# Pairs of heads in a two-block kernel: state steps 1 to 6 in place of 0 to 7, and VectorE's mean and variance of the last pair behind the level's subtractions

## The chip, the cores and the metric

The kernel runs on one core of one Trainium2 chip. The metric is the device time of one execution in microseconds (us); the median of three runs is given. TensorE is PE in the profile (PEld is its weight loads), VectorE is DVE, ScalarE is ACT, GpSimd is POOL, SyncE is SP.

## What is computed

`x` (1, 256, 2048) goes through two layers of a first block (gated linear attention, gated delta rule, differential attention) and then through a second block. The second block mixes its tokens by three parts side by side, and the first of them, 16 heads of 64 channels, is what the change touches. It scans the context (256 tokens) and then the sequence (256 tokens), forwards and backwards, all in float32:

```
def step(s, inp):
    r_t, w_t, k_t, v_t, kk_t, a_t = inp
    sa = jnp.einsum('bhij,bhj->bhi', s, -kk_t)
    s = (s * w_t[:, :, None, :] + sa[..., None] * (kk_t * a_t)[:, :, None, :]
         + v_t[..., None] * k_t[:, :, None, :])
    return s, jnp.einsum('bhij,bhj->bhi', s, r_t)
...
y = yf + yb
mu = jnp.mean(y, axis=-1, keepdims=True)
var = jnp.mean(jnp.square(y - mu), axis=-1, keepdims=True)
y = ((y - mu) * lax.rsqrt(var + GN_EPS) * ln_w + ln_b)
y = y + jnp.sum(r * (kf + kb) * r_k, axis=-1, keepdims=True) * v
return y * (jax.nn.sigmoid(gd) @ g_up), (sf, sb)
```

The context's scan starts from a state of zeros; the sequence's scan starts from the context's last state. Only the sequence's `y` is used. An output projection, a gated feed-forward part and a last norm follow.

## The kernel before

The second block's heads are worked off two at a time: `NP2 = 8` turns `j`, one for each pair, in five hand-written programs (`pairs_pe`, `pairs_act`, `pairs_dve` and parts of the POOL and SP programs) that run side by side and meet in semaphores. Every engine runs its own program in the written order, so an instruction that waits holds all that is written behind it on its engine. `d` is the direction (0 forwards, 1 backwards).

The 512 tokens of a pair are eight cells of 64, cells 0 to 3 of the context and 4 to 7 of the sequence, in the order of the direction. One turn does, in this order:

- **levels 1 to 5**: the inverse of each cell's triangular matrix, by doubling. For each level PE multiplies masks by the inverse so far (line 1843, "the first products"), ACT copies the result, PE multiplies again (lines 1856 and 1858, "the second products"), and DVE subtracts the result from the inverse and its transpose (lines 2517 and 2518, for each of the two directions: four subtractions a level). POOL makes the masks of levels 2 to 5 (line 1472).
- **the last pair's end**: `y` of pair `j - 1` is finished between the levels of turn `j`. PE's `head_means` (lines 1866 to 1869) stands behind level 1 and `head_vars` (line 1874) behind level 2. On DVE `centred` (it subtracts the mean; lines 2523 and 2525, the first shown as L2436) stands ahead of level 1's subtractions, `variances` (line 2530) ahead of level 2's, and `normed` (lines 2535 to 2541) ahead of level 3's. On ACT `squares` (line 2150) stands behind the copies of level 1 and `head_roots` (line 2154) behind those of level 2. POOL loads the pair's gate weights (line 1463) when `normed` is done, and makes the masks of levels 4 and 5 behind that.
- **`solved` and `steps`**: for each cell the matrix `step` and the addend `Z` of the state's recurrence.
- **the states**: a chain over cells. `GS[m + 1] = decay[m] * (step[m] x GS[m]) + Z[m]`. PE's `state(j, m)` is four products (two halves for each direction, line 1939), DVE's `state(j, m)` two small instructions (line 2564, shown as L2436 with 128x64). There are eight such steps, m = 0 to 7; `GS[0]` is set to zero by a memset on DVE (line 2556).
- **the next pair's streams**: DVE makes the backward inputs of pair `j + 1` in six parts (`stream(j + 1, 1, part)`), one behind each of the state's steps 0 to 5; the last part is line 2487. PE turns these inputs by `by_token(j + 1, r)` (lines 1788 and 1789): r = 0 and 1 stand behind steps 1 and 3, r = 2 behind the last step, r = 3 behind `outputs`. r = 2 needs the part of line 2487.
- **`outputs`**: PE multiplies `GS[4]` to `GS[7]` by the queries (line 1949), DVE gathers `y` (lines 2572 and 2574).

The last turn (j = 7) has no next pair. It has instead four large DVE sums over the mixed rows (`mix_sums`, lines 2332 to 2337) behind level 3's subtractions.

Of the kernel before, what the change touches and what calls it, by code (L numbers as in the profile page):

```python
# [1254 lines left out]
def second_block(nc, ctx, A, B, out):  # L1255
# [489 lines left out]
    def pairs_pe(pe):  # L1745
# [189 lines left out]
        def state(j, m):  # L1935
            for d in range(2):
                need("p_state", j, count(m + 1, d))
                for hs in halves:
                    mm = pe.matmul(PS[hs, d, cell(m)], step[d][hs, m, :], GS[d][hs, m, :], start=True, stop=True)
                done(mm, "p_gs")  # L1940

        def outputs(j):
            need("p_ypre", j, 1)
            for d in range(2):
                need("p_state", j, count(9, d))
# [15 lines left out]
        for j in range(NP2):  # L1961
# [461 lines left out]
    def pairs_dve(v, mix_sums):  # L2423
# [452 lines left out]
```

How the kernel before makes its waits and increments, by code:

```python
    def need(self, sig, k):  # L193
        self.eng.wait_ge(sig.sem, k + sig.start if self.turn is None else sig.at(self.turn, k))
# [6 lines left out]
    def settle(self):  # L201
        self.eng.wait_ge(self.last.sem, self.last.start + self.mark)
# [92 lines left out]
    def sp_program(sp):  # L296
        for n in range(NMOD1):
            if n >= RING:
                sp.wait_ge(vec_done.sem, n - RING + 1)
            sp.dma_start(ring[:, n % RING].rearrange("p k n -> p (k n)"), A["w_start"][n]).then_inc(opened[n % RING].sem, 16)
            if n % 2 == 0:
                i = n // 2
                if i > 1:
                    sp.wait_ge(S("aside_used").sem, i - 1)
                load[i % 2].inc(sp.dma_start(aside(i).rearrange("p c t n -> p (c t n)"), A["w_aside"][i]), 16)
        for l in range(NL):
            for t in range(0 if l else NSIDE, TILES1):
                if l or t > NSIDE + 1:
                    sp.wait_ge(tiles_done.sem, tiles_done.at(l, t - 1))
                else:
                    sp.wait_ge(vec_done.sem, (16, 14)[t % 2])
                load[t % 2].inc(sp.dma_start(ring[:, t % 2].rearrange("p k n -> p (k n)"), A["w_first"][l][t]), 16)
# [2 lines left out]
    def pool_program(pool):  # L315
# [8 lines left out]
        for l in range(NL):  # L324
            for i in range(VEC0[l], VEC0[l + 1]):
                pool.wait_ge(vec_done.sem, vec_done.start + (-1 if i < 2 else i - 2 if l == 0 else max(i - 1, VEC0[1])))
                half_loaded[half_place(i)].inc(pool.dma_start(half_slot(i), A["w_vec"][i]), 16)
```

## Time and profile before

| | us |
|---|---|
| median of 3 runs | 3397.76 (3395.79 to 3398.54) |
| the profiled execution, its own time | 3396.16 |
| its span in the trace | 3394.3 |
| the eight turns, in the trace | about 1855 to 2406, some 550 of the span |
| PE busy, share of the span | 92% |
| DVE busy | 47% |
| ACT busy | 16% |
| POOL busy | 33% |

The first block ends and the second block's input products run before the turns; its output projection and feed-forward part run behind them, with PE busy in nine tenths or more. In the turns PE is busy in seven to eight tenths, and they move next to nothing from memory. A turn takes some 70 us. Times of the trace are counted from the start of the span.

### The profile page before, as it was taken

How to read it: one execution, taken by the hardware profiler on the slowest of the kernel's cores; microseconds unless marked ns; L12 is line 12 of the kernel's file. 1: busy time of each engine (PE TensorE's matmuls, PEld its weight loads, DVE VectorE, ACT ScalarE, POOL GpSimd, SP SyncE). 2: the span in 40 equal slices, each digit the busy share in tenths (PEclk: the TensorE clock that was granted, in tenths of full speed). 3: DMA queues.
4: the chain of work that ended last, by engine and by line, in shares of the span. 5: the costliest groups of instructions: out<-in, count | busy, mean ns of one | idle time of the engine just before them, and what ended most of it. 6: DMA issues, size and time to landing. Idle time of an engine off the chain costs nothing.

```text
span 3394.3 us, 69586 instructions
## 1 busy us (share of the span) xinstructions
PE 3112.3 (92%) x32190; PEld 2794.7 (82%) x32190; DVE 1596.5 (47%) x2384; ACT 544.6 (16%) x1022; POOL 1109.8 (33%) x621
## 2 busy tenths in 40 slices
PE   5998999998999999999896888777999999999998
PEld 4877887877878888687895777666889999999998
DVE  4745275455437610587814666666334442113111
ACT  1012112021210111100003443343010000000001
POOL 1000000000000010243671211112447797778774
PEclk8998999998999999999997999999899999999999
DMA  7955387765335643477640000000445654444443
GB/s 281 405 224 198 120 316 286 306 246 205 107 145 216 231 177 139 172 274 288 250 150 11 10 7 7 7 7 6 162 149 224 227 221 170 161 167 162 162 166 109
DMA packets 56035, 583.10 MB, mean 172 GB/s; under 512 B 7314, under 2 KB 9680, under 8 KB 10816
## 3 DMA queue, kind: packets, MB, share of 16 engines
q1 hardware_dynamic: 37808, 465.06, 36.7%
q0 software_dynamic: 17936, 113.59, 8.8%
q8 instruction: 253, 4.15, 0.5%
q14 instruction: 38, 0.31, 0.0%
HBM read 576.52 MB, written 2.10 MB: 170 GB/s over the span
## 4 chain that ended last, share of the span: by engine, by line
PE 70%; DVE 13%; DMA 9%; issue 3%; ACT 3%; POOL 2%; SPq 0%; ACTq 0%; DVEq 0%; POOLq 0%
PE PS L1675 24%; PE PS L374 14%; PE PS L672 7%; PE PS L1628 5%; DMA ring<-in_w_vec_dram 5%; DMA ring<-in_w_second_dram 2%; DVE ring L2244 2%; PE PS L417 2%; PE PS L1843 1%; DMA ring<-in_w_start_dram 1%; PE PS L371 1%; PE PS L1856 1%; PE PS L1692 1%; PE PS L1611 1%; PE PS L1888 1%
## 5 line engine op out<-in xcount | busy, mean ns | idle before, releaser
L374 PE MATMUL PS<-H,ring 128*128 128x256 f32 x2944 | 669.4, 386 | 7.0 <-ACT H L702 7.0
L374 PEld LDWEIGHTS PS<-H,ring 128*128 128x128 f32 x2944 | 562.6, 193 | 95.0 <-issue 17.6
L1675 PE MATMUL PS<-H,ring 128*128 128x128 f32 x3424 | 404.5, 276 | 1.5 <-DMA ring<-in_w_second_dram 1.5
L1675 PEld LDWEIGHTS PS<-H,ring 128*128 128x128 f32 x3424 | 394.7, 193 | 2.4 <-DMA ring<-in_w_second_dram 1.9
L2351 DVE TENSOR_TENSOR W<-W,PS 128x256 f32<-128x256 f32 x58 | 24.4, 421 | 679.8 <-ACT W L2001 679.7
L327 POOL DMA_DIRECT2D ring<-in_w_vec_dram x75 | 39.7, 530 | 923.9 <-DVE ring L888 785.7
L1675 PE MATMUL PS<-H,W 128*128 128x128 f32 x2624 | 316.6, 276 | 8.4 <-POOL W L1504 7.2
L1675 PEld LDWEIGHTS PS<-H,W 128*128 128x128 f32 x2624 | 305.0, 193 | 9.7 <-POOL W L1504 8.0
L1499 POOL TENSOR_TENSOR W<-ring 128x1024 f32<-128x1024 f32 (+1 forms) x74 | 179.7, 2429 | 265.7 <-PE PS L1675 149.2
L672 PE MATMUL PS<-H,ring 128*128 128x256 f32 x1024 | 223.5, 379 | 2.9 <-DVE H L1174 2.9
L672 PEld LDWEIGHTS PS<-H,ring 128*128 128x128 f32 x1024 | 194.2, 190 | 29.9 <-issue 3.7
L1472 POOL TENSOR_TENSOR ring<-ring,W 128x512 f32<-128x512 f32 x64 | 84.9, 1342 | 367.1 <-PE PS L1843 366.7
L888 DVE SCALAR_TENSOR_TENSOR ring<-ring,H 128x2048 f32<-128x2048 f32 x75 | 171.1, 2287 | 29.3 <-DMA ring<-in_w_vec_dram 28.6
L1504 POOL TENSOR_TENSOR W<-ring,W 128x1024 f32<-128x1024 f32 (+1 forms) x74 | 182.4, 2465 | 5.8
L1502 POOL TENSOR_TENSOR W<-W,ring 128x1024 f32<-128x1024 f32 (+1 forms) x74 | 181.6, 2455 | 0.0
L1501 POOL TENSOR_TENSOR ring<-ring 128x1024 f32<-128x1024 f32 (+1 forms) x74 | 177.4, 2398 | 5.8
L1628 PE MATMUL PS<-H,ring 128*128 128x128 f32 (+1 forms) x992 | 142.5, 306 | 9.8 <-DMA ring<-in_w_second_dram 4.9
L1628 PEld LDWEIGHTS PS<-H,ring 128*128 128x128 f32 x992 | 134.4, 199 | 16.5 <-issue 5.7
L2244 DVE SCALAR_TENSOR_TENSOR ring<-ring,W 128x2048 f32<-128x2048 f32 x48 | 127.2, 2666 | 38.5 <-DMA ring<-in_w_vec_dram 38.0
L2001 ACT ACTIVATE W<-PS 128x128 f32<-128x128 f32 (+2 forms) x61 | 18.6, 307 | 786.1 <-PE PS L1675 777.3
L1675 PE MATMUL PS<-Pj,ring 128*128 128x128 f32 x1184 | 139.8, 275 | 3.3 <-DVE H L2337 3.3
L1675 PEld LDWEIGHTS PS<-Pj,ring 128*128 128x128 f32 x1184 | 135.9, 192 | 3.5 <-issue 3.5
(500 smaller groups left out, 4990.5 us busy)
## 6 DMA issues: line engine op xcount, KB each, us to landing
ring<-in_w_second_dram SPq DMA_DIRECT2D x97, 2048.0 KB, 8.1
ring<-in_w_first_dram SPq DMA_DIRECT2D x68, 2048.0 KB, 8.3
ring<-in_w_vec_dram POOLq DMA_DIRECT2D x75, 1024.0 KB, 7.8
ring<-in_w_vec_dram SPq DMA_DIRECT2D x48, 1024.0 KB, 5.1
ring<-in_w_start_dram SPq DMA_DIRECT2D x16, 2048.0 KB, 15.7
H<-in_w_vec_dram POOLq DMA_DIRECT2D x21, 1024.0 KB, 8.1
Pj<-in_w_aside_dram SPq DMA_DIRECT2D x8, 2048.0 KB, 11.2
ring<-in_w_second_dram SPq DMA_DIRECT2D x9, 1536.0 KB, 6.6
```

What stands on the lines that cost most here:

```text
L374: mm = pe.matmul(PS[:, t % 2, half * T:(half + 1) * T], ring[:, t % 2, k, half * P:(half + 1) * P], hT[:, k, :], start=(k == 0), stop=(k = ...
L417: mm = pe.matmul(PS[:, t, half * T:(half + 1) * T], left, right, start=(k == 0 and half == 0), stop=(k == KC - 1), skip_group_check=True)
L672: mm = pe.matmul(PS[:, 4 + 2 * (n % 2) + half, 0:T], ring[:, t % 2, k, half * P:(half + 1) * P], hT[:, k, :], start=(k == 0), stop=(k == K ...
L888: return v.scalar_tensor_tensor(out, a, s, b, op0, op1, **kw)
L1472: S("p_mask").inc(pool.tensor_tensor(mT[d], aT[d], Ci(f"c_join{lev}").unsqueeze(1).to_broadcast([P, 8, CH]), ALU.mult))
L1499: sums.inc(pool.tensor_tensor(s_[:, 0], quarter(q, 2, nk), quarter(q, 3, nk), ALU.add))
L1501: sums.inc(pool.tensor_tensor(quarter(q, 2, nk), quarter(q, 0, nk), quarter(q, 2, nk), ALU.subtract))
L1502: sums.inc(pool.tensor_tensor(s_[:, 1], s_[:, 0], quarter(q, 0, nk), ALU.subtract))
L1504: sums.inc(pool.tensor_tensor(s_[:, 2], quarter(q, 1, nk), s_[:, 1], ALU.subtract))
L1628: mm = pe.matmul(in_regions(n % 2, wide, r), w[:, k * P:(k + 1) * P], at(m, k), start=(k == 0 and r // per not in opened), stop=(k == 7), ...
L1675: mm = pe.matmul(regions(bank2, r), w[:, k * P:(k + 1) * P], m[:, k, :], start=(first and k == 0 and r // 4 not in opened), stop=(last and ...
L2244: v.scalar_tensor_tensor(w, w, 1.0, crow2[:, 0, :], ALU.mult, ALU.mult, accum_out=mod2[:, i - 64, 0:1]).then_inc(vec_done.sem, 1)
```

## The change

The state's steps 0 and 7 are left out. `GS[0]` is zero, so step 0 gives `GS[1] = Z[0]`: PE's step 1 reads `Z[0]` directly, and DVE's memset and its step 0 go. Step 7 gives `GS[8]`, which nothing reads. Six steps are left, m = 1 to 6; the six parts of the next pair's stream stand behind them one by one, `by_token` 0 and 1 behind the second and the fourth of them, and `by_token` 2 behind the last.

On DVE `centred` moves from ahead of level 1's subtractions to behind them, and `variances` from ahead of level 2's to behind them. PE's, ACT's and POOL's programs keep their order.

```diff
         def state(j, m):
             for d in range(2):
-                need("p_state", j, count(m + 1, d))
+                if m > 1:
+                    need("p_state", j, count(m - 1, d))
                 for hs in halves:
-                    mm = pe.matmul(PS[hs, d, cell(m)], step[d][hs, m, :], GS[d][hs, m, :], start=True, stop=True)
+                    mm = pe.matmul(PS[hs, d, cell(m)], step[d][hs, m, :], GS[d][hs, m, :] if m > 1 else Z[d][hs, 0, :], start=True, stop=True)
                 done(mm, "p_gs")
...
         def outputs(j):
             need("p_ypre", j, 1)
             for d in range(2):
-                need("p_state", j, count(9, d))
+                need("p_state", j, count(6, d))
...
             steps(j)
-            for m in range(8):
+            for m in range(1, 7):
                 state(j, m)
-                if after and m in (1, 3):
-                    by_token(j + 1, m // 2)
+                if after and m in (2, 4):
+                    by_token(j + 1, m // 2 - 1)
             if after:
                 by_token(j + 1, 2)
...
-            o.do(v.memset(GS[d][:, 0, :], 0.0), S("p_state"))
             need("p_reff", j, d + 1)
...
         def state(j, m):
             o = Order(v, own, j)
             for d in range(2):
-                need("p_gs", j, count(m + 1, d))
+                need("p_gs", j, count(m, d))
...
             starts(j)
+            level(j, 1)
             if before:
                 centred(j - 1)
-            level(j, 1)
+            level(j, 2)
             if before:
                 variances(j - 1)
-            level(j, 2)
...
-            for m in range(8):
+            for m in range(1, 7):
                 state(j, m)
-                if after and m < 6:
-                    stream(j + 1, 1, m)
+                if after:
+                    stream(j + 1, 1, m - 1)
```

The diff also changes the two counts of a turn that the semaphores of these steps reach. Lines behind 1937 are one higher in the changed kernel, up to the memset that is gone.

The order of VectorE from the end of level 1's starting values to level 2's subtractions, in a turn that has a pair before it. Before (`centred` is the pair of rows L2436 and L2525, `variances` L2530, the subtractions L2517 and L2518):

```order
L2504 TENSOR_TENSOR ring<-PS,W 128x512
L2436 SCALAR_TENSOR_TENSOR Pj<-PS,Pj 128x256
L2525 TENSOR_TENSOR Pj<-PS,Pj 128x256
L2517 TENSOR_TENSOR ring<-ring,PS 128x512
L2518 TENSOR_TENSOR ring<-ring,PS 128x512
L2517 TENSOR_TENSOR ring<-ring,PS 128x512
L2518 TENSOR_TENSOR ring<-ring,PS 128x512
L2530 TENSOR_SCALAR Pj<-PS 128x256
L2517 TENSOR_TENSOR ring<-ring,PS 128x512
L2518 TENSOR_TENSOR ring<-ring,PS 128x512
```

In the changed kernel (the same instructions, lines one higher):

```order
L2505 TENSOR_TENSOR ring<-PS,W 128x512
L2518 TENSOR_TENSOR ring<-ring,PS 128x512
L2519 TENSOR_TENSOR ring<-ring,PS 128x512
L2518 TENSOR_TENSOR ring<-ring,PS 128x512
L2519 TENSOR_TENSOR ring<-ring,PS 128x512
L2437 SCALAR_TENSOR_TENSOR Pj<-PS,Pj 128x256
L2526 TENSOR_TENSOR Pj<-PS,Pj 128x256
L2518 TENSOR_TENSOR ring<-ring,PS 128x512
L2519 TENSOR_TENSOR ring<-ring,PS 128x512
L2518 TENSOR_TENSOR ring<-ring,PS 128x512
L2519 TENSOR_TENSOR ring<-ring,PS 128x512
L2531 TENSOR_SCALAR Pj<-PS 128x256
```

`centred` and `variances` each moved behind four subtractions; nothing else on VectorE moved there.

VectorE at the end of the state's chain, in a turn with a next pair. Before (the 128x64 rows are the state's steps, L2480 to L2487 parts 3 to 5 of the next pair's stream, L2572 the start of `outputs`):

```order
L2480 TENSOR_TENSOR W<-W 128x512
L2436 SCALAR_TENSOR_TENSOR Pj<-PS,H,ring 128x64
L2436 SCALAR_TENSOR_TENSOR H<-PS,H,ring 128x64
L2482 TENSOR_TENSOR Pj<-W,Pj 128x256
L2483 COPY H<-W 128x8
L2436 SCALAR_TENSOR_TENSOR Pj<-PS,H,ring 128x64
L2436 SCALAR_TENSOR_TENSOR H<-PS,H,ring 128x64
L2487 TENSOR_TENSOR W<-W 128x512
L2436 SCALAR_TENSOR_TENSOR Pj<-PS,H,ring 128x64
L2436 SCALAR_TENSOR_TENSOR H<-PS,H,ring 128x64
L2436 SCALAR_TENSOR_TENSOR Pj<-PS,H,ring 128x64
L2436 SCALAR_TENSOR_TENSOR H<-PS,H,ring 128x64
```

In the changed kernel:

```order
L2481 TENSOR_TENSOR W<-W 128x512
L2437 SCALAR_TENSOR_TENSOR Pj<-PS,H,ring 128x64
L2437 SCALAR_TENSOR_TENSOR H<-PS,H,ring 128x64
L2483 TENSOR_TENSOR Pj<-W,Pj 128x256
L2484 COPY H<-W 128x8
L2437 SCALAR_TENSOR_TENSOR Pj<-PS,H,ring 128x64
L2437 SCALAR_TENSOR_TENSOR H<-PS,H,ring 128x64
L2488 TENSOR_TENSOR W<-W 128x512
L2572 COPY Pj<-PS 128x2x2x64
```

The four rows behind the stream's last part are gone: that part, and no longer a step of the state, is now the last thing ahead of `outputs`.

## Rows read from the trace of the kernel before

**Rows 1.** The page: the span.

```profile
span 3394.3 us, 69586 instructions
```

**Rows 2.** Three windows: length; busy PE, PEld, DVE, ACT, POOL; clock; DMA share; GB/s.

```profile
1925.00:1995.00 70.00, 56.24 (x1794) 48.79 (x1794) 46.67 (x96) 28.44 (x52) 12.43 (x11) 0.98 0.03 8
2135.00:2206.00 71.00, 58.84 (x1796) 51.47 (x1795) 46.63 (x96) 28.48 (x52) 12.55 (x11) 0.92 0.03 8
2346.00:2410.00 64.00, 46.91 (x1246) 40.34 (x1245) 37.15 (x72) 12.27 (x25) 9.85 (x7) 0.84 0.21 80
```

**Rows 3.** Waits in the turns: who waited, for whom, us in total, times, longest.

```profile
PE PS L1843 <- DVE ring L2517: 18.0, 15, 2.6
...
PE PS L1858 <- issue: 8.3, 9, 2.0
PE PS L1856 <- issue: 7.6, 8, 1.3
```

**Rows 4.** Timeline of PE, levels 1 to 3 of turn 3: start, us, instruction, wait before it.

```profile
2063.10 1.03 PE L1869 MATMUL PS<-Pj,W 128*128 128x256 f32 x4
2065.79 2.29 PE L1843 MATMUL PS<-ring 64*64 64x64 f32 x62 [1.66 <-DVE ring L2517]
...
2070.49 0.70 PE L1874 MATMUL PS<-Pj,con 128*128 128x256 f32 x2
2071.03 0.95 PE L1768 MATMUL PS<-con,W 128*128 128x2 f32 x8
2072.39 0.29 PE L1843 MATMUL PS<-ring 64*64 64x64 f32 x3 [0.42 <-DVE ring L2517]
```

**Rows 5.** Timeline of DVE in the same stretch.

```profile
2064.16 0.42 DVE L2436 SCALAR_TENSOR_TENSOR Pj<-PS,Pj 128x256 f32<-128x256 f32 x1 [4.91 <-PE PS L1869]
...
2071.23 0.42 DVE L2530 TENSOR_SCALAR Pj<-PS 128x256 f32<-128x256 f32 x1 [3.79 <-PE PS L1874]
...
2076.85 0.42 DVE L2541 TENSOR_TENSOR H<-Pj,PS 128x256 f32<-128x256 f32 x1
```

**Rows 6.** Timeline of ACT in that stretch, and of POOL.

```profile
2064.62 0.42 ACT L2097 ACTIVATE Pj<-Pj 128x256 f32<-128x256 f32 x1 [6.41 <-DVE Pj L2436]
2066.98 0.60 ACT L2097 ACTIVATE ring<-PS 128x512 f32<-128x512 f32 x1 [1.94 <-PE PS L1843]
...
2071.68 0.42 ACT L2097 ACTIVATE Pj<-Pj 128x256 f32<-128x256 f32 x1 [1.61 <-DVE Pj L2530]
2073.58 0.60 ACT L2097 ACTIVATE ring<-PS 128x512 f32<-128x512 f32 x1 [1.48 <-PE PS L1843]
```

```profile
2077.57 0.75 POOL L1463 DMA_DIRECT2D W<-in_g_up_dram  x1 [8.04 <-DVE H L2541]
2078.34 2.50 POOL L1472 TENSOR_TENSOR ring<-ring,W 128x512 f32<-128x512 f32 x2
```

**Rows 7.** Timelines of DVE and PE, end of the state's chain in turn 3.

```profile
2111.15 0.68 DVE L2487 TENSOR_TENSOR W<-W 128x512 f32<-128x512 f32 x1
...
2112.67 0.27 DVE L2436 SCALAR_TENSOR_TENSOR H<-PS,H,ring 128x64 f32<-128x64 f32 x1
```

```profile
2112.09 0.33 PE L1939 MATMUL PS<-Pj,ring 64*64 64x64 f32 x4 [0.46 <-DVE Pj L2436]
...
2112.54 0.33 PE L1788 MATMUL PS<-con,W 128*128 128x128 f32 x1
```

**Rows 8.** Timeline of PE in the last turn: waits of levels 3 and 4, end of the chain.

```profile
2355.95 2.29 PE L1843 MATMUL PS<-ring 64*64 64x64 f32 x62 [1.20 <-DVE ring L2517]
...
2363.16 2.31 PE L1843 MATMUL PS<-ring 64*64 64x64 f32 x62 [2.26 <-POOL ring L1472]
...
2391.72 0.33 PE L1939 MATMUL PS<-Pj,ring 64*64 64x64 f32 x4 [0.20 <-DVE Pj L2436]
...
2392.44 0.33 PE L1939 MATMUL PS<-Pj,ring 64*64 64x64 f32 x4 [0.19 <-DVE Pj L2436]
...
2394.98 1.12 PE L1949 MATMUL PS<-Pj 64*64 64x64 f32 x16 [0.27 <-DVE Pj L2436]
```

More of the change, by code:

```diff
@@ new lines @@
+PER_TURN = {'load0': 304, 'load1': 304, 'load2': 0, 'tiles_done': 38, 'evac0': 19, 'evac1': 19, 'pair_end': 1, 'vec_done': 48, 'half0_loaded': 304, 'half1_loaded': 296, 'half2_loaded': 168, 'open0_loaded': 0, 'open1_loaded': 0, 'open2_loaded': 0, 'in_loaded': 16, 'aside_used': 0, 'dl_out': 1, 'p_y': 2, 'y_scaled': 2, 'out_stored': 64, 'y_scaled_act': 2, 'const_loaded': 16, 'c_loaded': 16, 'pos_loaded': 16, 'small_loaded': 320, 'heads_loaded': 64, 'wsm_loaded': 32, 'wlr_loaded': 16, 'narrow': 1, 'crow_loaded': 0, 'mix_ready': 4, 'ctx_loaded': 16, 'rows_zero': 1, 'vec_loaded': 352, 'c2_loaded': 16, 'at_rec': 2, 'ff_sum': 372, 'h_scaled': 16, 'h_scaled_2': 32, 'mix_rest': 4, 'cells_loaded': 16, 'pair_loaded': 32, 'gla_z': 1, 'p_z': 2, 'dl_P0': 6, 'p_P': 10, 'gla_ln': 1, 'p_mask': 8, 'gate_loaded': 16, 'at_root': 2, 'ff_t': 2, 'c3_loaded': 16, 'x_T': 8, 'x_copied_dve': 4, 'x_copied_act': 4, 'vcol_T': 0, 'x_sq': 8, 'x_ssq': 1, 'h_ready': 16, 'lam_prod': 1, 'lam_sum': 1, 'nar_copied': 1, 'nar_T': 1, 'gla_kt': 1, 'gla_ktT': 1, 'gla_scores': 1, 'dl_glog': 1, 'dl_gcum': 1, 'gla_ktok': 1, 'gla_ds': 1, 'gla_att': 1, 'gla_state': 1, 'gla_out': 1, 'dl_ug': 1, 'dl_rows': 1, 'dl_sq': 4, 'gla_norm_in': 1, 'dl_ssq': 1, 'dl_rec': 1, 'dl_brow': 2, 'dl_nb': 1, 'dl_kb': 1, 'dl_kk': 1, 'dl_vs': 2, 'dl_vT': 1, 'dl_aT': 1, 'dl_vtok': 1, 'dl_A': 1, 'dl_kT': 1, 'dl_af': 2, 'dl_x0': 1, 'dl_mT0': 5, 'dl_mT1': 5, 'dl_P1': 6, 'dl_Pc0': 6, 'dl_Y0': 6, 'dl_Pc1': 6, 'dl_Y1': 6, 'dl_inv': 12, 'dl_v0': 1, 'dl_v0c': 1, 'dl_s1': 1, 'dl_s1c': 1, 'dl_ks': 1, 'dl_r1': 1, 'dl_v1': 1, 'dl_v1c': 1, 'o_sq': 2, 'o_ssq': 2, 'o_rec': 2, 'o_nb': 2, 'at_sq': 2, 'at_ssq': 2, 'o_normed': 1, 'at_nb': 2, 'at_normed': 2, 'at_rope': 1, 'at_scores': 8, 'at_max': 8, 'at_a': 4, 'at_aT': 4, 'at_aTc': 4, 'at_out': 4, 'sq_2': 24, 'ctx_T': 8, 'ctx_copied': 8, 'vec_T': 1, 'csq_2': 1, 'ssq_2': 4, 'h_ready_2': 32, 'in_t': 2, 'mod_done': 1, 'ft_1': 1, 'at_ms': 2, 'ft_copied': 2, 'ft_2': 1, 'lora_act': 2, 'p_ksq': 1, 'p_kssq': 1, 'dl_ms': 1, 'p_kms': 1, 'dl_dec': 1, 'p_sig': 4, 'gla_zb': 1, 'p_kbig': 1, 'p_kbc': 1, 'p_streams': 2, 'p_tokT': 4, 'p_tokc': 4, 'p_AX': 2, 'p_BR': 2, 'p_mT': 2, 'p_xt': 1, 'p_BRr': 2, 'p_Pc': 10, 'p_x0': 2, 'p_Y': 10, 'at_exp': 16, 'p_xm': 8, 'p_sub': 10, 'p_bv': 2, 'p_bvc': 4, 'p_u': 2, 'p_uc': 4, 'p_g': 2, 'p_rhs': 2, 'p_kk': 1, 'p_reff': 2, 'p_Zread': 2, 'p_rt': 2, 'p_ypre': 1, 'p_step': 2, 'p_gs': 12, 'p_state': 12, 'p_yread': 2, 'p_ysum': 1, 'p_mean': 1, 'dl_outc': 1, 'p_ysq': 1, 'p_var': 1, 'p_bg_read': 1, 'down_t': 3, 'y_ready': 8, 'y_T': 8, 'down_read': 8, 'out_turned': 8, 'act_start': 25, 'c_done': 1, 'ang_red': 2, 'rope_abs': 2, 'act_step': 29, 'x_ms': 1, 'x_root': 1, 'lam_exp': 1, 'gb_copied': 1, 'dl_z': 1, 'dl_ebeta': 1, 'dl_ln': 1, 'gla_cum': 1, 'gla_blast': 1, 'gla_exps': 8, 'dl_gcr': 2, 'dl_eg': 2, 'dl_diff': 1, 'dl_root': 1, 'o_ms': 2, 'o_root': 2, 'c_next': 0, 'c_last': 1, 'ms_2': 4, 'root_2': 4, 'c_scaled': 1, 'ff_first': 77, 'in_conv': 11, 'mix_ft': 1, 'p_act': 14, 'p_kroot': 1, 'p_krec': 1, 'p_tm': 2, 'p_cs': 2, 'p_exp': 2, 'p_yc': 1, 'p_vms': 1, 'p_vroot': 1, 'x_new': 16, 'c_again': 1, 'ff_prod': 22, 'ff_silu': 21, 'rs_ready': 1, 'dve_start': 393, 'dve_step': 200, 'vec_copied': 4, 'p_dve': 28, 'p_ak': 2, 'p_kd': 2, 'p_bonus': 2}
```

1 line of the change is left out of this document (removed).

## The prediction

> **What bounds the kernel now.** I read the page first: the span is 3394.3 us, and the execution's own time 3396.16 lies 1.9 above it [rows 1]. The median of the runs shown, 3397.76, lies 1.6 above the profiled execution. Then the windows of single turns: PE is busy for 56.24 of 70 us, DVE for 46.67, ACT for 28.44, and memory moves 8 GB/s [rows 2]. So no engine is full in the turns; they are a chain that passes from engine to engine, and what counts is which wait ends last at each place. The list of waits names the one that the change touches most: PE's first products of a level wait 18.0 us for DVE's subtractions [rows 3]. The timelines then say what DVE was doing while PE waited.
>
> **Part 1, `centred` behind level 1's subtractions.** In turn 3 PE ends `head_means` at 2063.10 + 1.03 = 2064.13 and then stands for 1.66 us until DVE has subtracted [rows 4]. DVE had nothing to do for 4.91 us before `centred`, since `centred` waits for `head_means` and the subtractions are queued behind it [rows 5]; their own input, level 1's second products, stands ahead of `head_means` on PE. With the subtractions first they run inside those 4.91 us (four, of which `centred`'s end at 2065.04 and PE's start at 2065.79 bound the first at 0.75), and PE goes from `head_means` straight into level 2: 1.66 us gone. Who waits for the moved `centred`? It starts when `head_means` ends, as now. ACT's `squares` runs at 2064.62 + 0.42 = 2065.04 and the first copy of level 2, queued behind it, is wanted when PE's first half of level 2 is done. That copy now starts at 2066.98 [rows 6], so with PE 1.66 earlier at 2065.32: 0.28 us of room. Cost nothing, and at most some tenths if that room is used up.
>
> **Part 2, `variances` behind level 2's subtractions.** DVE waits 3.79 us for `head_vars` with level 2's subtractions behind it [rows 5], and PE, done with `head_vars` and the next pair's key sums at 2071.98, waits 0.42 us for the first of them [rows 4]. That goes. What is late next: `variances` follows the subtractions; the second products of level 2 end near `head_vars`' start, 2070.49 - 1.66 = 2068.83, two subtractions follow to about 2070.1, then `variances` to 2070.5, and ACT's root to 2071.0. That root stands ahead of ACT's copies of level 3, whose first is now at 2073.58 [rows 6] and would be wanted at 2073.58 - 2.08 = 2071.50: 0.5 us of room. DVE's `normed` follows the root; from the root's end 2071.68 + 0.42 = 2072.10 to the end of `normed`, 2077.27, there are 5.2 us today, of which DVE spends the first 1.9 on level 2's subtractions, which will lie ahead of it. It would end at 2071.0 + 3.3 = 2074.3, 2.9 us earlier than now. POOL's gate load and first mask of level 4 hang on it: 2077.57 to 2078.34 + 1.25 = 2079.6 today [rows 6], about 2076.7 then, against level 4's start that only moves by 2.08. So POOL's cover grows.
>
> **Sum of parts 1 and 2.** The 15 waits of 18.0 us are seven of 1.66, six of 0.42 (turns 1 to 6), 1.20 in the last turn at level 3, and one of about 2.6 at level 5 of the last turn behind `mix_sums`, which stays. Removed: 7 x 1.66 + 6 x 0.42 + 1.20 = 15.3 us. In the last turn level 4 waits 2.26 us for POOL's mask [rows 8]; the mask hangs on `normed`, which moves by the same 2.9 us as PE, so the gain is kept, and `mix_sums` starts as much earlier.
>
> **Part 3, six state steps.** In a turn with a next pair the last step's DVE instruction ends at 2112.67 + 0.27 = 2112.94, two steps of about 0.85 us behind the stream's last part [rows 7]. One would think that 1.7 us go. But the six stream parts still stand one behind each of six steps, so the last part still ends where it ends now, at 2111.15 + 0.68 = 2111.83, and PE's `by_token` 2, written ahead of `outputs`, needs it. Today `by_token` 2 starts at 2112.54 [rows 7]; it will start at about 2111.89 (DVE's end plus the 0.06 us by which PE follows DVE in these steps). Gain 0.65 us in each of seven turns, 4.5 us. The rest of the removed steps was, and will be, beside the stream. The last turn has no stream: its steps follow each other at 0.72 us, one at 2391.72, the sixth at 2392.44, and from there to `outputs` at 2394.98 are 2.54 us for three steps' DVE part and two steps' PE part [rows 8]. Two steps of 0.72 are 1.44; the remaining 1.1 can't all be the last DVE instruction, whose start is about 0.8 behind its PE part, so these steps ran slower than 0.72 each. Gain between 1.4 and 1.8 us, I take 1.6. Sum 6.1 us.
>
> **Part 4, small ones.** The two memsets per turn stand in DVE's queue ahead of a wait, and DVE starts the next instruction 0.03 us behind each; 0.2 us over the kernel, between 0 and 0.9. PE's eight fewer products per turn (each stands as two matmuls and two weight loads in the trace) lie in stretches where PE waits for DVE: nothing. Reading `Z` in place of `GS` adds no wait, since PE's last wait before the chain is for DVE's instruction that stands behind it.
>
> **What eats into the sum.** PE also stands for "issue", with no releaser: 8.3 us in 9 places on line 1858 and 7.6 in 8 on line 1856 [rows 3], the second products, where its instructions are shortest. Where a stop fell inside a wait that goes now, it shows. I take 1 us, between 0 and one such stop (0.9 us) per turn, 7 us. [...]
>
> **The sum.** 15.3 + 6.1 + 0.2 - 1 = 20.6 us. Against the profiled execution 3396.16 - 20.6 = 3375.6; against the median 3397.76 - 20.6 = 3377.2. I predict 3377 us, 0.6% less.
>
> **Rivals.**
> (a) The waits come back as stops. One more stop of 0.9 us per turn, or POOL's masks holding level 4: if the root on ACT came so late that `normed` did not move, level 4's mask would end at 2079.6 as now, where PE would want it at 2077.9, and most of the 2.08 us of a turn were lost. For it: only 0.28 and 0.5 us of room on ACT. Against it: `normed` is worked out 2.9 us earlier. Time 3384 to 3390.
> [...]
> [...]
> (d) It does not do what it says: `head_means`, and not DVE, is what level 2 waits for. Then part 1 gives nothing: 3377 + 11.6 = 3389. But PE's row says DVE for all 1.66 us.
>
> **How the numbers follow.** Forecast, 3372 to 3382: 0.66. (a) and (d), 3382 to 3391: 0.17. (b), under 3372: 0.10. Within 0.2% of before (6.8 us, about what a measurement of this kernel can tell from no change), from (a) with (c) partly: 0.04. (c): 0.03. Faster by over 0.2% is then 0.93, same 0.04, slower 0.03. The range takes (b)'s time and half of (a): 3369 to 3387.
>
> **What would show it.** In the changed kernel PE's wait ahead of level 2's first products is gone behind `head_means` (under 0.2 us), and that of level 3 too; `by_token` 2 starts right behind the end of the stream's last part; ACT's `squares` and root stand before the copies without PE waiting for them; the last turn has `outputs` about 1 us behind its sixth step. A turn is 67.3 us long where its clock is 0.98. The prediction is wrong if "issue" on lines 1856 and 1858 grows by more than 5 us, if PE waits for ACT at levels 2 or 3, or if the turns' mean clock changes by more than 0.02.

## The result: 36.9 us less, where 20.6 were forecast

The changed kernel takes 3361.3 us (median of 4 runs, 3359.2 to 3364.0), the kernel before in the same comparison 3398.2 us: a ratio of 0.9892, 95% interval 0.9875 to 0.9909. The direction was forecast, the size was not: 3377 was said, and 3361.3 lies below the range of 3369 to 3387. The spans of the two profiled executions differ by the same 36.9 us, 3394.3 [rows 1] and, on the page of the changed kernel:

```profile
span 3357.4 us, 69274 instructions
```

Nearly the whole difference, 35.0 us, arises in the turns. From the first product of `scores` of the first pair to the first product behind the turns the kernel before takes 562.3 us and the changed kernel 527.3. What lies ahead of them is the same work in both and is 3.1 us shorter in this pair of profiles (1842.8 and 1839.7 us); what lies behind is 989.2 us in the one and 990.4 in the other. The windows of that stage (columns as in [rows 2]), the kernel before first, then the changed kernel:

```profile
1842.80:2405.10 562.30, 449.92 (x14297) 393.93 (x14296) 366.96 (x745) 213.24 (x391) 98.74 (x84) 0.95 0.04 12
```

```profile
1839.70:2367.00 527.30, 438.65 (x14169) 386.58 (x14168) 361.99 (x698) 213.85 (x391) 98.34 (x84) 0.95 0.04 13
```

In this pair of profiles the granted clock is 0.95 in both, 57 us at the lower of its two levels before and 53 after; more runs show a larger difference (see "The clock" below). The two levels are 1.00 and 0.50: the granted clock is 1.00 over 2346 to 2356 us of the kernel before and 0.50 over 2394 to 2398. Line 1869's four matmuls take 1.03 us at the upper level [rows 4] and 1.91 us at the lower (at 2400.26). PE is busy for 11.3 us less although only 128 small matmuls (of 14,297) are gone, and it stands still for 23.7 us less.

The list of PE's waits in the turns of the changed kernel, to be held against [rows 3] (who waited, for whom, us in total, times, longest):

```profile
PE PS L1856 <- DVE ring L2437: 19.1, 8, 2.4
PE PS L1788 <- DVE W L2488: 8.3, 7, 1.2
...
PE PS L1843 <- POOL ring L1472: 5.2, 7, 3.0
...
PE PS L1843 <- DVE ring L2518: 3.1, 1, 3.1
...
PE PS L1856 <- issue: 2.8, 5, 1.4
```

The wait of the first products for DVE has one case left, the one of level 5 in the last turn behind `mix_sums` (2.6 us before, 3.1 now); 14 of 15 are gone. "Issue" on line 1856 fell from 7.6 to 2.8 us, and line 1858 is not in the list of the changed kernel at all (8.3 us before). These are the stops that the prediction expected to grow. On some other lines "issue" did grow: from 2.6 to 4.5 us on line 1829 and from 1.3 to 3.9 on line 1908. The wait for POOL's masks grew too; before, its row was:

```profile
PE PS L1843 <- POOL ring L1472: 3.0, 3, 2.3
```

Turn 3 of the changed kernel on PE, levels 1 to 4, against [rows 4]:

```profile
2050.71 1.03 PE L1869 MATMUL PS<-Pj,W 128*128 128x256 f32 x4
2051.67 2.08 PE L1843 MATMUL PS<-ring 64*64 64x64 f32 x63
...
2055.96 0.70 PE L1874 MATMUL PS<-Pj,con 128*128 128x256 f32 x2
2056.50 0.95 PE L1768 MATMUL PS<-con,W 128*128 128x2 f32 x8
2057.38 2.08 PE L1843 MATMUL PS<-ring 64*64 64x64 f32 x63
...
2063.85 1.15 PE L1843 MATMUL PS<-ring 64*64 64x64 f32 x32 [0.35 <-POOL ring L1472]
```

Level 2's first products follow `head_means` with no wait, level 3's follow the key sums with none. Two things beside that were not in the forecast. The group of first products, 62 matmuls in 2.29 us before, is 63 in 2.08 us now. And level 4 waits 0.35 us for POOL.

DVE in that stretch, against [rows 5]:

```profile
2049.84 0.69 DVE L2518 TENSOR_TENSOR ring<-ring,PS 128x512 f32<-128x512 f32 x1 [0.42 <-PE PS L1858]
2050.44 0.68 DVE L2519 TENSOR_TENSOR ring<-ring,PS 128x512 f32<-128x512 f32 x1
2051.78 0.42 DVE L2437 SCALAR_TENSOR_TENSOR Pj<-PS,Pj 128x256 f32<-128x256 f32 x1 [0.66 <-PE PS L1869]
```

The four subtractions now lie in what was idle time, and `centred` still starts as `head_means` ends. At the chain's end (against [rows 7]), DVE and then PE:

```profile
2095.68 0.68 DVE L2488 TENSOR_TENSOR W<-W 128x512 f32<-128x512 f32 x1
```

```profile
2096.42 0.33 PE L1788 MATMUL PS<-con,W 128*128 128x128 f32 x1 [1.19 <-DVE W L2488]
```

`by_token` 2 starts 0.06 us behind the end of the stream's last part, as worked out. In the last turn (against [rows 8]) the sixth step and `outputs` are 0.81 us apart:

```profile
2356.29 0.33 PE L1940 MATMUL PS<-Pj,ring 64*64 64x64 f32 x4 [0.19 <-DVE Pj L2437]
...
2357.10 1.12 PE L1950 MATMUL PS<-Pj 64*64 64x64 f32 x16 [0.28 <-DVE Pj L2437]
```

So every wait that should go went, and 14 to 16 us more went than was forecast. The experiments look for those.

### The profile page after: what moved, and what is told of

Read it like the earlier page. It is cut to its first block, busy times and chain, and to the rows that moved or that the text cites. A ratio compares the mean times of both kernels' runs of the same rounds, so it can differ in the third digit from the quotient of the medians.

```text
span 3357.4 us, 69274 instructions
## 1 busy us (share of the span) xinstructions
PE 3095.8 (92%) x32062; PEld 2782.9 (83%) x32062; DVE 1601.0 (48%) x2336; ACT 545.2 (16%) x1022; POOL 1106.2 (33%) x621
## 3 DMA queue, kind: packets, MB, share of 16 engines
q1 hardware_dynamic: 37808, 465.06, 36.9%
## 4 chain that ended last, share of the span: by engine, by line
PE 69%; DVE 14%; DMA 9%; ACT 3%; issue 3%; POOL 2%; SPq 0%; ACTq 0%; DVEq 0%; POOLq 0%
PE PS L1675 24%; PE PS L374 14%; PE PS L672 7%; DMA ring<-in_w_vec_dram 5%; PE PS L1628 5%; PE PS L417 2%; DMA ring<-in_w_second_dram 2%; DVE ring L2245 2%; PE PS L371 1%; PE PS L1856 1%; DMA ring<-in_w_start_dram 1%; PE PS L1692 1%; PE PS L1843 1%; DVE ring L888 1%; PE PS L1611 1%
## 5 line engine op out<-in xcount | busy, mean ns | idle before, releaser
L1675 PEld LDWEIGHTS PS<-H,W 128*128 128x128 f32 x2624 | 303.3, 192 | 10.2 <-POOL W L1504 8.6
L888 DVE SCALAR_TENSOR_TENSOR ring<-ring,H 128x2048 f32<-128x2048 f32 x75 | 171.1, 2287 | 28.6 <-DMA ring<-in_w_vec_dram 27.7
```

The costliest lines, as they stand in the source:

```text
L888: return v.scalar_tensor_tensor(out, a, s, b, op0, op1, **kw)
L1675: mm = pe.matmul(regions(bank2, r), w[:, k * P:(k + 1) * P], m[:, k, :], start=(first and k == 0 and r // 4 not in opened), stop=(last and ...
```

## Experiments

Two theories stood at the start. **A, place:** the stops called "issue" come at the boundaries of blocks of 256 PE instructions, and six steps in place of eight moved these boundaries to better places. That the stops lie there is in the traces (all but up to 1.3 us of them in a profile of the turns, see the last section); that PE stops because its next block has not arrived is a reading. **B, lead:** a stop grows where PE had just waited for another engine, so the stops went with the waits. That PE then has no instructions queued was the author's assumption; no view shows how many PE has in hand. Comparisons are with the kernel before on the same chip; as its median moved between 3394 and 3403 us from one comparison to the next, the ratios are compared. "Stops" are below the idle times of PE of over 0.1 us at a boundary for which the trace names no other engine.

### The two halves of the change

e1: the kernel before with DVE's order alone changed. PE's instruction stream is exactly that of before.

```
             starts(j)
+            level(j, 1)
             if before:
                 centred(j - 1)
-            level(j, 1)
+            level(j, 2)
             if before:
                 variances(j - 1)
-            level(j, 2)
```

> The kernel before with `centred` and `variances` behind the subtractions, and nothing else: all eight state steps stay, and TensorE's instructions are the same, one for one, as before. What is to be told apart is why the unexplained stops of TensorE (31.3 us of 'issue' in the turns before, 18.2 in the changed kernel) became fewer. Theory A (place): every stop stands where TensorE's instruction stream crosses from one block of 256 to the next, since the next block has not arrived; which stretches of a turn get such a crossing depends on the number of instructions ahead of it, and this kernel has the number of before. Then the waits for VectorE go (15.3 us), and the 0.22 us by which TensorE's two halves of the first products were spread in levels 2 and 3 (14 times, 3 us), and the stops stay at 28 to 36 us: some 18 us faster than before, ratio 0.9947. Theory B (lead): the stops are shown only where TensorE had just been waiting for VectorE and had no instructions queued; without those waits they shrink here as well: issue 18 to 22 us and 28 to 31 us faster, ratio 0.991.

Measured: 3364.2 us, ratio 0.9908 (0.9893 to 0.9922), 30 us less; the turns 538.0 us, 24.3 less, with 10 us more at the lower clock level. PE's stream had not moved by one instruction, so the place can't have given this. The stops fell to 25.8 us from 30.6: the time is the one that theory B gave, the stops lie between B's 18 to 22 and A's 28 to 36.

e2: the changed kernel with that DVE order put back, six steps alone.

> The changed kernel with `centred` and `variances` back ahead of the subtractions: only the six state steps remain. TensorE's instructions are those of the changed kernel, 3587 in a turn in place of 3620. Theory A (place): the stops fall as in the changed kernel, to about 20 us of issue, so 6 us from the shorter chain and 8 to 13 us from the stops: 14 to 19 us faster than before, ratio 0.995. Theory B (lead): the waits for VectorE at levels 2 and 3 are as before, so the stops stay at about 31 us and the gain is 6 us, ratio 0.998.

Measured: 3390.3 us, ratio 0.9985 (0.9974 to 0.9996), 4 to 5 us less, 7.4 us in the turns. This is the part whose place of boundaries changed, and it gave about the 6.1 us of its steps. Its stops are 27.7 us, 3 us less than before, where A had said 20. The two ratios multiply to 0.9893, that of the whole; in single profiles of the turns the halves give 24.3 + 7.4 = 31.7 of 35.0 us.

The changed kernel and e2 differ in DVE's order alone, so they too have one PE stream. From e2 to the changed kernel the turns are 27.6 us shorter and the stops 10.2 us less (24.9 and 6.6 with the second profile of the changed kernel, below). That is e1's result again, at the other place of the boundaries.

### Part 1 and part 2 apart

e5: the kernel before with `centred` alone behind level 1's subtractions. e6: with `variances` alone behind level 2's.

> The kernel before with centred alone behind level 1's subtractions (variances stays between the two levels' subtractions, as before). Theory L (a stop goes with the wait of its own level): level 2 loses the wait of 1.66 us, 0.22 us of its first products and some of the stop in its second products, in each of seven turns; level 3 keeps its wait of 0.42 us, and its second products stay at about 3.4 us. Time 3394 - 13 - 5 = 3376 us, 3373 to 3379. Theory S (stops hang on the whole schedule and not on the wait of a level): level 3's second products fall to about 2.1 us here too, and the time is 3368 to 3372 us. By the terms of the prediction alone (11.6 us) it would be 3382.

> The kernel before with variances alone behind level 2's subtractions (centred stays ahead of level 1's). Theory L: level 2 keeps its wait of 1.66 us and its second products their 2.7 to 3.6 us; level 3 loses 0.42 us of wait, 0.22 us of its first products, and its second products fall from 3.4 to about 2.1 us. Time 3394 - 3.7 - 1.4 - 6 = 3383 us, 3381 to 3386. Theory S: only wait and first products give, 5 us: 3388 to 3390 us, with second products of 3 us and more left at level 3.

Measured: e5 3378.5 us, ratio 0.9940 (0.9924 to 0.9957), about 20 us less, the turns 14.9 us shorter, the stops 27.8 us; e6 3387.1 us, ratio 0.9966 (0.9950 to 0.9983), about 12 us less, the turns 9.3 us shorter, the stops 27.2 us. 14.9 + 9.3 = 24.2, e1's 24.3. In e5 the second products of level 2 fell to 2.08 us in five of the turns 1 to 7 (2.1 to 3.5 before), while those of level 3 stayed at 3.2 to 3.9 us in turns 2 to 5: as theory L said. In e6 level 3's should have fallen to 2.1 and did not, 3.0 to 3.6 us in turns 2 to 5 (3.3 to 3.6 before), though the wait ahead of them was gone. Only in turns 6 and 7 did they fall, from 2.7 and 2.8 to 2.1 us. There L fails in most turns, although e6's 12 us agree with the 11 that it gave: the wait of 0.42 us that went took a part of the stop behind it at most.

### The pacing of the first products

e7: the kernel before, with the subtractions of levels 1 and 2 in another order.

```
                 if lev < 5:
                     o.do(v.tensor_tensor(xm[d], xm[d], bankv(2 + d), ALU.subtract), S("p_xm"))
-                o.do(v.tensor_tensor(xmT[d], xmT[d], bankv(4 + d), ALU.subtract), S("p_sub"))
+                if lev not in (1, 2):
+                    o.do(v.tensor_tensor(xmT[d], xmT[d], bankv(4 + d), ALU.subtract), S("p_sub"))
+            if lev in (1, 2):
+                for d in range(2):
+                    o.do(v.tensor_tensor(xmT[d], xmT[d], bankv(4 + d), ALU.subtract), S("p_sub"))
```

> The kernel before, in which VectorE at levels 1 and 2 subtracts xm of both directions first and xmT of both behind them, in place of one direction after the other; nothing else. The pacing term: level 2's and level 3's first products take 1.86 us in place of 2.08, since PE's second half no longer waits for the third subtraction. 14 x 0.22 = 3.1 us less: 3391 us, with the waits of 1.66 and 0.42 us unchanged. Rival: what the first products gain comes back ahead of the second products, as a wait for the last subtraction or as a longer stop: 3394 us. It can be told from the trace even where the times can't.

Measured: 3393.6 us, ratio 0.9986 (0.9972 to 1.0000). Too close to 1 for the time alone, but the trace tells it. Level 2's first products in turn 2 of e7:

```profile
1995.08 2.06 PE L1843 MATMUL PS<-ring 64*64 64x64 f32 x63 [1.66 <-DVE ring L2517]
```

The wait is still 1.66 us, and the group is 2.06 us long where it was 2.29 in [rows 4]. From first to second products it is 1.85 us in place of 2.08 at both levels. DVE's instructions start every 0.6 us (2049.84 and 2050.44 in the rows of the changed kernel above), and `xm` of direction 1 is the third; PE's first half takes 0.93 us in e7 (ACT's two copies of its results start at 1996.30 and 1997.23) and had to wait for it. That wait stood inside a group and had no line in any list. It is worth 14 x 0.22 = 3.1 us, and the new order removes it, since all four subtractions are done before PE comes. e7's turns last 553.4 us in its profile, 8.9 less than before and not 3.1; 1.4 us of that are fewer stops (29.2), and it spent 12 us less at the lower clock level, some 5 us at 0.4 us each. This 0.4 is an estimate, used below as well: at the level of 0.50 a busy PE does about half of its work (1.03 and 1.91 us for the same four matmuls), and PE is busy for 449.92 of 562.30 us, 0.80.

### Where the boundaries lie

e3: the changed kernel with 32 products (128 instructions) once ahead of the turns. e4: the changed kernel with eight unread products behind the sixth step of each turn, so that PE's stream has as many instructions per turn as before.

> The changed kernel with 32 small products (64x64, 128 instructions of TensorE) more, once, ahead of the turns, where TensorE waits for ScalarE; their result is not used. They cost at most 1 to 2 us. Theory A (place): in every turn the crossings of blocks lie 128 instructions elsewhere, so the places of the stops in a turn all change and their sum with them, by 5 us or more in either direction, most likely up (the changed kernel has few): 3363 to 3380 us. Theory B (lead): places and sum of the stops stay as in the changed kernel (18 us), 3361 to 3364 us.

> The changed kernel with eight products that nothing reads behind the sixth state step of every turn, where the removed steps stood: TensorE's stream has exactly the instructions of before again (16304 products and 471 waits), at the same places. In a turn the products cost about 0.25 us in front of by_token 2, 2 us in all. Theory A (place): the stops are those of before, about 31 us of issue, so 12 us or more of the changed kernel's gain are lost: 3373 to 3378 us. Theory B (lead): the stops stay at 18 us: 3363 us.

Measured: e3 3367.1 us, ratio 0.9914 (0.9896 to 0.9933); e4 3361.9 us, ratio 0.9904 (0.9884 to 0.9923). e4 is as B said (23.4 us of stops, less than A's 31 and more than B's 18). e3 is not: its median lies in A's range of 3363 to 3380 and above B's 3361 to 3364, and its stops are 33.8 us where B said 18, though its turns, 526.9 us, are as long as the changed kernel's. So where the boundaries lie does move the stops, and more shifts were needed.

a2 and b2: both kernels a second time, for second profiles. e9 and e13: the changed kernel with 16 and 48 products ahead of the turns (64 and 192 instructions). e10 and e11: the kernel before and e1, each with the 16 products.

> The changed kernel again, for a second profile of it. Theory F (fixed by the program): the stage of the turns lasts 527.3 us again within 2, with 18.5 us of stops at PE's block boundaries within 2. Theory V (it varies from execution to execution): more than 5 us of difference in one of the two. Time 3361 us, ratio 0.989.

> The kernel before again, for a second profile of it. Theory F: the turns last 562.3 us again within 2, with 30.9 us of stops within 2, and 58 us at the lower clock. Theory V: more than 5 us of difference in one of them, and then the 12 us by which the stops of the changed kernel are fewer are partly luck of two profiles. Time 3397 us, ratio 1.000.

> The changed kernel with 16 more products of 64 x 64 once ahead of the turns (64 instructions of PE, a quarter of a block), so that every boundary of 256 instructions lies elsewhere in each turn. Theory A (the place of the boundaries decides the sum): the stops change from 18.5 us by more than 8, and the turns by as much: time off 3361 by more than 6 us. Theory B (stops and waits for VectorE trade places): the stops may change, but the turns last 527 us within 3 once the lower clock is allowed for at 0.4 us each, and the time is 3361 us within 4.

> The changed kernel with 48 more products ahead of the turns (192 instructions, three quarters of a block). With 0, 64 and 128 it took 3362, 3353 and 3367 us. The changed kernel's boundaries keep their place from turn to turn (3587 is 14 blocks and 3), so each place has its own time: between 3353 and 3368 us, most likely 3360. Rival (the 10 us of the first shift are not place): 3362 us within 2, as unshifted.

> The kernel before with 16 more products of 64 x 64 once ahead of the turns, so that PE's block boundaries lie 64 instructions elsewhere. Drift theory: before's turns have 3620 instructions, 14 blocks and 36, so that the boundaries pass through nearly all places in seven turns, and a shift changes little: 3398 us, within 4; turns 563 us. Rival (place decides for this kernel too, as for the changed one): 3387 us or less, or 3405 and more.

> The kernel before with both of DVE's steps moved (eight state steps kept) and with the same 16 products ahead of the turns. Theory W (the surplus goes with the waits): 29 us less than the shifted kernel before, 25 to 33, so about 3368 us. Theory P (it was the place): 18 us less or little more, the 15.3 of the waits and 3.1 of the pacing, so about 3379 us.

The last column is the time that the turns spent at the lower clock level.

| kernel | ratio | turns, us | stops, us | lower level, us |
|---|---|---|---|---|
| before, twice | 1 and 0.9999 | 562.3 and 563.0 | 30.6 and 28.8 | 57 and 66 |
| before, shift 64 (e10) | 0.9996 | 568.8 | 32.8 | 71 |
| changed, twice | 0.9892 and 0.9893 | 527.3 and 530.0 | 17.5 and 21.1 | 53 and 49 |
| changed, shift 64 (e9) | 0.9860 | 521.0 | 24.7 | 43 |
| changed, shift 128 (e3) | 0.9914 | 526.9 | 33.8 | 32 |
| changed, shift 192 (e13) | 0.9902 | 533.4 | 29.2 | 45 |
| changed, as many instructions as before (e4) | 0.9904 | 524.7 | 23.4 | 37 |
| order only (e1) | 0.9908 | 538.0 | 25.8 | 67 |
| order only, shift 64 (e11) | 0.9913 | 541.6 | 25.4 | 64 |
| six steps only (e2) | 0.9985 | 554.9 | 27.7 | 53 |

Read from this:

1. Second profiles differ by 0.7 and 2.7 us in the turns, by 2 to 4 us in the stops and by 4 to 9 us at the lower level, so theory F's 2 us was too narrow, and a difference under 3 us in one profile is nothing.
2. The changed kernel depends on the place, but not through the sum of its stops. With shift 64 it took 3352.9 us where the unshifted one took 3363.3 on the same chip, and 6 to 9 us of that are in the turns; its stops rose, by 4 to 7 us. What made it faster isn't shown. Of theory A's two signs for e9 the time came true (over 6 us off 3361) and the stops did not (over 8 us of change). e13 was forecast at 3353 to 3368 us and took 3369.8, on a chip on which the kernel before took 3403.4.
3. The kernel before is not measurably moved by the same shift: e10's median is 3400.9 us where 3398 within 4 was forecast, and its turns are 568.8 us, not 563. Its turns have 3620 instructions in the trace (matmuls, weight loads and PE's waits on semaphores), 14 blocks and 36, so its boundaries drift through the turn; the changed kernel has 3587, 14 blocks and 3, and its boundaries stay.
4. The unshifted changed kernel is no lucky place: its ratio is the mean of the four. e4, whose boundaries drift like those of the kernel before, has 0.9904, with about 2 us of added products in it.
5. e11 against e10 is again a pair with one PE stream: 28 us less by the medians, 27.1 in the turns. Theory W, said to give 25 to 33, holds; P, 18, does not. The stops are 7.4 us less.
6. The sum of stops alone does not set the length: e3 has 13 to 16 us more of them than the changed kernel and equal turns, with about 20 us less at the lower clock level.

### The stops, boundary by boundary

The boundary is every 256th instruction of PE's stream, the one position modulo 256 at which the stops of all 17 profiles lie (last section). As before and e1 have one stream, each boundary can be compared with itself. In turn 2 of the kernel before a boundary is crossed at 1996.52, shortly behind the wait of 1.66 us; the next is where PE stops:

```profile
1996.20 2.28 PE L1843 MATMUL PS<-ring 64*64 64x64 f32 x62 [1.66 <-DVE ring L2517]
...
2000.84 0.27 PE L1856 MATMUL PS<-ring 64*64 64x64 f32 x2 [1.25 <-issue]
```

The view of the DMA over 1996 to 2001 us, 40 slices of 0.125 us, has one packet, of the queue that carries instructions:

```profile
DMA  0000000000000000000400000000000000000000
...
q8 instruction: 1, 0.02, 1.2%
```

It starts at about 1998.4, 1.9 us behind the first boundary, and PE resumes 2.4 us behind the packet's start. In e1 the same stretch of the program lies at 1983 to 1988 us, the first boundary at 1984.67:

```profile
1983.63 0.81 PE L1869 MATMUL PS<-Pj,W 128*128 128x256 f32 x3
1984.38 2.08 PE L1843 MATMUL PS<-ring 64*64 64x64 f32 x63
```

```profile
DMA  0000040000000000000000000000000000000000
```

The packet is there at 1983.7, before the boundary, and the stop of 1.25 us is 0. Now all turns, with the stops added up at the second boundary behind each of the 14 removed waits, the one that stops in this example, and at the 98 or 99 others:

| pair with one PE stream | those 14, us | the others, us |
|---|---|---|
| before, first profile, and e1 | 8.4, then 3.4 | 22.2, then 22.4 |
| before, second profile, and e1 | 8.4, then 3.4 | 20.4, then 22.4 |
| e10 and e11 | 6.2, then 4.3 | 26.6, then 21.1 |
| e2 and changed, first profile | 6.9, then 1.4 | 20.8, then 16.1 |
| e2 and changed, second profile | 6.9, then 3.1 | 20.8, then 18.0 |

So part of the surplus is shown: 2 to 5.5 us of stops hung on the waits themselves. The other boundaries changed by anything from 5.5 us less to 2 us more, and no pair tells why. In the example the packet of the next block starts late counted from the boundary, and where the block is one of dense 64 x 64 products (256 instructions in 2.1 us: the second products of level 2 in e1, 1986.23 to 1988.32), PE arrives first. That the wait is what delays the packet is my reading of these pairs. It isn't the only cause: in e1, where these waits are gone, stops of up to 1.7 us are left.

### A faster version

e8: in the changed kernel three of the six stream parts of direction 1 move into DVE's idle time ahead of the chain.

```
+            if after:
+                stream(j + 1, 1, 0)
+                stream(j + 1, 1, 2)
             steps(j, 0)
             steps(j, 1)
+            if after:
+                stream(j + 1, 1, 1)
             for m in range(1, 7):
                 state(j, m)
-                if after:
-                    stream(j + 1, 1, m - 1)
+                if after and m < 4:
+                    stream(j + 1, 1, m + 2)
```

e12: the same, with the 16 products ahead of the turns.

> The changed kernel with three of the six parts of direction 1's stream moved into DVE's idle time ahead of the state chain: two of them ahead of the chunk steps (idle of 1.48 us in the changed kernel), one between them and the chain (idle of 1.46 us); the other three stand behind the first three state steps. Theory (DVE's last stream part holds PE's by_token 2, 1.19 us of wait at its end): by_token 2 then waits for ACT's copy of by_token 1, or for the sixth step; it starts about 1.5 us earlier in each of seven turns, 10 us: 3361 - 10 = 3351 us, 3349 to 3355. Rival: the parts ahead of the chunk steps and of the chain make PE wait there for DVE by what they overrun the idle time, and ACT's copy comes as late as now: 3357 to 3363 us.

> The kernel with three stream parts moved earlier, with the same 16 products ahead of the turns. If the two gains add, 3351 - 10 = 3341 us, 3338 to 3346; if earlier parts and shift remove the same stops, 3348 to 3352 us.

Measured: e8 3350.8 us, ratio 0.9860 (0.9841 to 0.9878); e12 3349.5 us, ratio 0.9836 (0.9816 to 0.9857). The end of the chain in turn 3 of e8, on PE:

```profile
2086.83 0.33 PE L1940 MATMUL PS<-Pj,ring 64*64 64x64 f32 x4 [0.27 <-DVE Pj L2437]
2087.02 0.33 PE L1940 MATMUL PS<-H,ring 64*64 64x64 f32 x4
2087.45 0.30 PE L1788 MATMUL PS<-con,W 128*128 128x128 f32 x1
```

The wait of 1.19 us ahead of `by_token` 2 is gone, and from the chain's start to `outputs` it is 1.22 us less in five turns, 1.55 and 0.66 in the other two, where 1.5 had been forecast. These rows give 8.3 us. Its turns last 511.0 us, 16.3 less than in the first profile of the changed kernel, with 17 us less at the lower clock level (37 in place of 53); by the ratios the gain is 11 us. Whether the shift adds to it is open: the intervals overlap, and e12's turns lasted 516.7 us in its one profile, with 30.9 us of stops against e8's 17.6.

## Where the prediction was right, and where it fell short

**Bound and places: right.** The turns are a chain of waits, and the edits acted at the places that were named.

**Parts 1 and 2: right, undersized.** The waits of 15.3 us went in full, and `centred`, ACT's `squares` and root delayed nobody at levels 2 and 3. From `head_means` to level 2's first product it is 1.73 us less, at level 3 0.49 us less, 0.07 more each than the waits of 1.66 and 0.42: 14 x 0.07 = 1.0 us. The pacing of the first products, 3.1 us, was not in the sum.

**POOL's cover: wrong.** `normed` did move forward, but level 4 comes forward by more, since level 3's second products lost their stops (2.08 us in turns 1 to 7; up to 3.6 before). PE's wait for the masks grew from 3.0 us in 3 places to 5.2 in 7. The wait in the last turn, where the gain was to be kept, went from 2.26 to 3.0 us.

**Part 3: right.** 0.65 us a turn and 1.8 in the last, 6.35 us, against 6.1; e2 gave 7.4 in the turns.

**"What eats into the sum": the step that failed.** I took 1 us of loss, up to 7, for stops that come back. The stops fell instead, 30.6 to 17.5 us in the first pair of profiles, 28.8 to 21.1 in the second, 10.4 on the mean. Most of that goes with DVE's order at an unchanged PE stream: 3.0 to 4.8 us from before to e1, 7.4 from e10 to e11, 6.6 to 10.2 from e2 to the changed kernel. From before to e2, where the boundaries moved and the waits stayed, it is 1 to 3 us. In the turns of the profiles here PE stood at 29 to 43 of some 112 boundaries for 0.1 to 2.0 us.

**The clock, (b) of the chances: set aside too early.** (b) stood for a PE that keeps its clock better and a time of about 3369 us, 8 us under the forecast; I gave it 0.10 and kept it out of the sum, while the low end of the range is its time. No run shows this term of 8 us by itself. What the runs show in its place is this. The first pair of profiles has 57 and 53 us at the lower level in the turns, but all three profiles of the kernel before have 57 to 71, and the six of the changed kernel, at any place of the boundaries, 32 to 53. The granted clock of every run says the same. As the lower level is 0.50, a run's time at it is twice (one less its clock) times its span: a2's four runs have 242 us of it, the 17 runs of the kernel before in the same comparison 263; e3, e4, e9 and e13 have 10 to 30 us less than theirs. That is 20 us on the mean of the five. With the order alone (e1 and e11) it is 9 to 13. Among the 70 runs of the kernel before, a run with 1 us more at the lower level is 0.35 us longer (fitted inside each comparison, standard error 0.03). So by an estimate from these two numbers, 20 x 0.35, some 7 of the 37 us come from the clock, near (b)'s 8. That shorter waits are what kept the clock up isn't shown; no run changes the clock alone.

**The sum again.** For the turns (means of two profiles each, 562.7 and 528.7): 15.3 + 1.0 + 3.1 + 6.35 + 10.4 (stops) - 2.2 (POOL) = 34 us, and 34.0 were measured. That they meet is partly luck, since the clock, 11 us less at the lower level in these profiles, adds some 4 us at 0.35 to 0.4 each. The terms are good to about 4 us together. With -1 for the stops, and neither the pacing nor the clock, the forecast had 20.6.

**Rivals.** (a), waits that come back as stops, fell by the opposite sign; its other half, POOL's masks holding level 4, cost the 2.2 us above. (b) came true in part, beside the forecast's own terms. (c), a kernel made slower by more time at the lower level, fell: the turns have 53 and 49 us of it, 57 and 66 before. (d) fell by the 1.73 us a turn.

**Open.** e1's time is 30 us less, its turns only 24.3 in one profile and 27.1 in the shifted pair; the start of the turns varies by 12 us between profiles of kernels with the same first block (1834.8 to 1847.3 us), so a single profile can't place the rest. Which place of the boundaries is best, what made shift 64 faster with more stops, and why e6 kept level 3's stops, isn't known.

## What to carry to other kernels

Where an engine waits in the middle of its densest stretch, look whether the wait is worth more than its row: here 15.3 us of rows were worth 24 to 28 in the turns, through stops at blocks of 256 instructions (2 to 5.5 us at the boundaries behind the waits), through a second, hidden wait inside the group of matmuls that follows (3.1 us), and, as far as the runs tell, through the clock (9 to 13 us less at the lower level in e1 and e11). The wait inside the group was found by comparing the group's length, 2.29 us, with its length where nothing holds it, 2.06 to 2.08. A change whose gain is under 10 us in a kernel with such stops should be tried with its instructions shifted, for one changed kernel had ratios of 0.9860 to 0.9914, 18 us apart, with nothing but unused products ahead of its loop. Whether the clock changed is not to be read from one pair of profiles: here that pair said 4 us at the lower level, and the granted clock of all runs said 20.

## What was not expected of the hardware

PE's stops called "issue" in the turns lie, but for up to 1.3 us of them in a profile, at one position modulo 256 of its instructions, the same in all 17 profiles. Matmuls, weight loads and PE's waits on semaphores have to be counted; without the waits the 38 stops of the kernel before lie at 29 different positions or more. There is one 16 KB packet of the instruction queue for each boundary (113 and 113 in the kernel before). In all 17 profiles together PE stops for 0.3 us or more at 510 boundaries, and at each of them such a packet starts 2.1 to 3.0 us before PE resumes. The traces thus tie the stops to these packets; that the packet carries the block that PE waits for is a reading. A block of 64 x 64 f32 products is run in 2.1 us (e1, level 2's second products). With the packet starting mostly 0.5 to 1.7 us behind the boundary before it, PE arrives early, by up to 2.0 us. The boundary of the example had its packet 1.9 us behind the boundary before it after a wait for DVE, and 1.0 us ahead of it without that wait.
